# A value projection between a tile's scores and their product, and a modulation step at the end of tile 0, in the mLSTM and retention heads

## The reference, cut to what matters

```python
qk = jnp.einsum('nbhtd,nbhsd->nbhts', qc, kc)                  # scores of a block
s = qk_c * jnp.exp(d_c - m_t[..., None])                       # mLSTM: scores times decay
num = einsum(s, v_c) + w_inter * einsum(q_c, C)                # product with the values, plus the carried state
C = dec * C + einsum(kw, v_c)                                  # the state takes in keys times values
o_intra = einsum(einsum(q, k) * dec_intra, v)                  # retention: the same with constant decays
mod = cs @ w_ada[l] + b_ada[l]                                 # modulation, one vector per layer and condition
```

## Time and profile before

| | |
|---|---|
| Time, median of 3 executions | 1649.74 us (1644.46 to 1652.1) |
| Profiled execution, its own time | 1651.91 us |
| Its span, first to last instruction | 1650.1 us |
| PE busy | 1537.0 us, 93% |
| DVE busy | 961.3 us, 58% |
| ACT busy | 627.9 us, 38% |
| Mean granted PE clock | 0.967 |

### The profile page before, as it was taken

How to read it: one execution, slowest core, us unless ns; L and a number is a source line. 1 busy time by engine, 2 the same in 40 slices (tenths; PEclk the granted TensorE clock), 3 DMA queues, 4 the chain that set the end, 5 groups by cost and what they waited for, 6 DMA issues and landing times. The chain is left out here.

```text
span 1650.1 us, 30954 instructions
## 1 busy us (share of the span) xinstructions
PE 1537.0 (93%) x11168; PEld 1433.2 (87%) x11168; DVE 961.3 (58%) x2118; ACT 627.9 (38%) x1491; POOL 181.0 (11%) x384
## 2 busy tenths in 40 slices
PE   6999999998999999899799999899999999977898
PEld 2689898987999999799698889889999999966898
DVE  2565555554766656643565555576677677663622
ACT  2522222222232222332554434254555555543521
POOL 1000000000000000000100010022223122312000
PEclk8999999999999999999899899999999999988999
DMA  9434333432551433133342213221111211020223
GB/s 326 116 100 104 95 104 94 109 88 48 126 153 46 140 95 109 48 99 92 118 81 73 67 43 80 73 65 47 50 48 43 70 43 54 5 72 2 89 87 115
DMA packets 195257, 140.89 MB, mean 85 GB/s; under 512 B 18332, under 2 KB 178584, under 8 KB 194916
## 3 DMA queue, kind: packets, MB, share of 16 engines
q1 hardware_dynamic: 177772, 130.16, 28.2%
q10 hardware_dynamic: 17400, 9.60, 2.0%
HBM read 128.58 MB, written 11.15 MB: 85 GB/s over the span
## 5 line engine op out<-in xcount | busy, mean ns | idle before, releaser
L180 PE MATMUL bank<-hT,w_high 128*128 128x288 f32 x1152 | 364.4, 316 | 6.7 <-ACT gla_ls_x L1195 2.4
L181 PE MATMUL bank<-hT,w_low 128*128 128x288 f32 x1152 | 345.6, 300 | 0.0
L182 PE MATMUL bank<-hT,w_high 128*128 128x288 f32 x1152 | 345.2, 300 | 0.0
L180 PEld LDWEIGHTS bank<-hT,w_high 128*128 128x128 f32 x1152 | 223.3, 194 | 9.0 <-ACT gla_ls_x L1195 2.6
L181 PEld LDWEIGHTS bank<-hT,w_low 128*128 128x128 f32 x1152 | 223.2, 194 | 0.0
L182 PEld LDWEIGHTS bank<-hT,w_high 128*128 128x128 f32 x1152 | 222.5, 193 | 0.0
L180 PE MATMUL bank<-output_w_split,gT_high 128*128 128x256 f32 x512 | 143.4, 280 | 0.0
L182 PE MATMUL bank<-output_w_split,gT_high 128*128 128x256 f32 x512 | 143.2, 280 | 0.0
L181 PE MATMUL bank<-output_w_split,gT_low 128*128 128x256 f32 x512 | 142.5, 278 | 0.0
L181 PEld LDWEIGHTS bank<-output_w_split,gT_low 128*128 128x128 f32 x512 | 96.8, 189 | 0.0
L180 PEld LDWEIGHTS bank<-output_w_split,gT_high 128*128 128x128 f32 x512 | 96.1, 188 | 0.1
(11 more groups left out here) (487 smaller groups left out, 3597.4 us busy)
## 6 DMA issues: line engine op xcount, KB each, us to landing
x<-in_w_in_even SPq DMA_DIRECT2D x72, 512.0 KB, 5.0
x<-in_w_in_odd SPq DMA_DIRECT2D x56, 512.0 KB, 4.1
x<-in_w_ada SPq DMA_DIRECT2D x32, 256.0 KB, 4.5
front_w_ada<-in_w_ada SPq DMA_DIRECT2D x6, 1024.0 KB, 14.8
output_w_raw<-in_w_out_even SPq DMA_DIRECT2D x12, 512.0 KB, 3.4
output_w_raw<-in_w_out_odd SPq DMA_DIRECT2D x12, 512.0 KB, 3.6
gdn_E<-G_rows SPq DMA_DIRECT2D x8, 576.0 KB, 5.0
gT<-in_w_ada SPq DMA_DIRECT2D x16, 256.0 KB, 4.0
```

The lines of the kernel that those rows point to most:

```text
L180: pe.matmul(out, w[0], x[1], start=first, stop=False)
L181: pe.matmul(out, w[1], x[0], start=False, stop=False)
L182: return pe.matmul(out, w[0], x[0], start=False, stop=last)
```

## The change

There are two edits. On PE, in tile 0 of an mLSTM head the value projection moves behind the scores and transposes, and in the first of these heads behind `pe_columns` as well. In a retention head the value projection of tile 0 stays, and that of tile 1 moves up from the beginning of tile 1 to the place behind the scores of tile 0; kind C is as before. On DVE, in a retention head the later step at the end of tile 3 is now at the end of tile 0. Steps are counted as they are issued, so step 4 is now the one at the end of tile 0, and steps 5, 6 and 7 take the places of 4, 5 and 6.

```diff
                         if t == 0:
                             project_gates(t)
                             pe.wait_ge(*v_low.done(h, NC - 1))
-                            project_v(t)
+                            if kind != "A":
+                                project_v(t)
                             if kind == "A" and previous is None:
                                 chain.pe_columns(pe)
                             pe.wait_ge(*(qk_copied.done(h, NP - 1) if kind == "A" else qk_ready.done(h, 0)))
-                        else:
+                        elif t > 1 or kind != "B":
                             project_v(t)
                         pe.wait_ge(*kw_ready.before(h, t))
...
                         last.then_inc(scores_psum.sem, 1)
+                        if t == 0 and kind != "C":
+                            project_v(1 if kind == "B" else 0)
                         if t:
                             project_gates(t)
...
-                        if kind == "B" and t == PT - 1:
+                        if kind == "B" and t == 0:
                             later_step(h)
```

## The result

The changed kernel took 1639.65 us (median of 8 executions, 1636.72 to 1641.2) against 1647.62 for the kernel before (8 executions, 1644.46 to 1652.1). The medians differ by 8.0 us. The ratio of the two kernels, which is not taken from these two medians, is 0.9946, with a 95% interval of 0.9936 to 0.9956: 8.9 us faster (7.2 to 10.5). Timed again in another job (the experiment before the last) it was 0.9934, 0.9920 to 0.9947: 10.9 us (8.7 to 13.2), with medians 12.2 apart. The forecast was 1638.7 and a gain of 11.0. The profiled execution took 1638.62, with a span of 1636.8 us.

What follows compares the result with a forecast made beforehand. PE, busy 93% of the span, was taken as the bound, so only its stalls and slow clock counted. Terms 3.3 + 4.4 + 0.4 + 2.9 = 11.0 us, off the median 1649.74, gave 1638.7, range 1635 to 1645.

Steps and rivals of the forecast that it cites:

- Retention, tile 0: Product of tile 0, four heads: tile 1's value matmuls fill PE's wait for the scores; 3.3 us gained.
- The new wait for ACT's copy: Retention tile 0: the moved projection overwrites bank 3 and waits for ACT's copy of the values; costs 0.08 per head.
- Retention, tile 1: Moved step on DVE ahead of tile 1's scores costs nothing, with 0.7 us of cover before the product.
- A flush behind the step: DVE after the moved step: by the skill page about 0.95 us more, overrunning cover by 0.25 a head; gain 10, not 11.
- The loads: Weight blocks of steps 4 to 7, needed about one tile earlier, still land in time; nothing is late.
- The rival of a late block: Retention: step 4's block has not landed when DVE needs it; 5 us late would give 1656; chance 0.03.
- Retention, tile 4: Product of the sample tile, four heads: its wait for v_sample goes once the step is moved; 4.4 us gained.
- mLSTM, heads 2 to 4: Product in tile 0: the wait for scores becomes one for ACT's value copy; 0.13 a head, 0.4 us gained.
- PE's reaction to ACT: PE's delay after the end of ACT's copy, taken as 0.09 us in sizing the waits on copied values.
- mLSTM, first head, directly: Product's wait stays at nearly 2 us because the load of negM bounds the chain; only 0.2 us gained.
- mLSTM, first head, the clock: A dense value block ahead of the wait keeps PE's higher clock level behind it; 2.7 us gained.
- the forecast's first rival: First mLSTM head: the clock still falls because the wait keeps its length; gain 8.3, 1641.4 us; chance 0.26.

Runs made afterwards that it cites:

- e2: Kernel before with only the retention value projection of tile 1 moved ahead of tile 0's product, later step left at tile 3: 1645.42 us, ratio 0.9970.
- e5: Changed kernel with two later steps at the end of tile 0 of a retention head and none in tile 1: 1642.38 us, ratio 0.9958 to the kernel before.
- e3: Kernel before with only the retention later step moved from the end of tile 3 to the end of tile 0, PE order unaltered: 1644.19 us, ratio 0.9967.
- e9: Changed kernel, unaltered, timed again beside the kernel before on the same chip: 1638.53 us against 1650.69, ratio 0.9934.
- e8: Kernel before, unaltered, profiled once more: 1645.48 us in its one execution.
- e1: Kernel before with only the mLSTM edit, tile 0's value projection behind the scores in all mLSTM heads: 1647.35 us, ratio 0.9986.
- e4: Kernel before with the new PE order in the first mLSTM head only: 1647.99 us, ratio 0.9992.
- e6: Changed kernel with mLSTM tile 0 also in retention order and ACT copying tile 0's values before the decays: 1633.93 us, ratio 0.9904 to the kernel before.

## Why the prediction was right, point by point

- **Retention, tile 0 (forecast 3.3).** Right. In the first head, from the scores of tile 0 to the product of tile 1 it was 10.00 before and is 442.01 - 432.79 = 9.22: 0.78, forecast 0.77. The other heads had idles of up to 0.7 before, and e2 shows 0.9 a head, 3.6 in all (0.1 of it was not in the forecast: in the first head the value block of tile 2 takes 443.45 to 446.26, 2.81, instead of 2.91, and why is open). The new wait for ACT's copy is there: the first value matmul starts 0.64 behind the start of the scores, against 0.59 without a wait.
- **Retention, tile 1 (nothing).** Right. The scores of tile 1 are done at 441.04, PE sees it by 441.24, and the product stands at 442.01: 0.77 of cover by the rows, 0.82 by e5, forecast 0.7.
- **A flush behind the step.** The successor of the moved step starts after 1.32 us of its 1.41, and after both pairs in e5 at 2.65 of 2.73. By the Trainium skill, VectorE: DVE Perf Modes, section "The DRAIN you can't avoid", a flush of about an operation's duration less 266 ns would have stood there. The trace after doesn't agree with the forecast's estimate from it, for at 0.95 more the product would have waited, and it did not. The same section adds that a next operation that is not held starts earlier, which the estimate left out; so this pair need not contradict it.
- **The loads (nothing).** Right. DVE went from `g` straight to the step, 0.41 apart, with no wait for a block. The rival of a late block is out.
- **Retention, tile 4 (4.4).** Right: 1.94 became 0.86, and e3 shows 1.2 a head, 4.8 in all. The three retention terms together were 7.7; the start of the heads moved from 402.06 to 399.07 and their last transposes from 685.79 to 674.58, so they gave 8.2. Most of the 0.5 more is the 0.1 a head named under tile 0.
- **mLSTM, heads 2 to 4 (0.4).** The mechanism was right, the size half of it. The wait moved to `mlstm_v` with an idle of 0.56. From the first gate matmul to the product the third head took 9.79 before and 9.72 after, the fourth 9.80 and 9.73: 0.07 a head, 0.2 in all. The step that was mis-sized is PE's reaction to ACT, taken as 0.09 from the first head. In the third head (ACT, then PE):

```profile
265.47 0.38 ACT L1247 ACTIVATE mlstm_v<-bank 128x256 f32<-128x256 f32 x1 [2.89 <-PE bank L182]
266.00 0.67 PE L173 MATMUL bank<-mlstm_v,mlstm_scores 128*128 128x257 f32 x2 [0.56 <-ACT mlstm_v L1247]
```

  PE's last value matmul began at 265.16, so a next one could have begun at 265.28; the copy started 0.19 later, where the forecast had 0.20, and took its 0.38. PE then began 0.15 after its end instead of 0.09, and that is the missing 0.06.
- **mLSTM, first head, directly (0.2).** 12.80 from the gates to the product became 12.69: 0.1, and 12.55 in e9, 0.3. The load bounded it, as forecast.
- **mLSTM, first head, the clock (2.7).** Right for the profile that the forecast read: 6.90 became 4.20. It was the least certain term, and it is shown by comparison: all four profiles in which the small transposes and scores stand right ahead of the wait (before, e2, e3, e8) have a fall to the 1.2 GHz level there, after an idle of 2.06. None of the five with the 24 value matmuls between them and a wait of 1.79 to 2.00 has one (after, e1, e4, e5, e9). That the gap alone lowers the clock, the forecast's first rival, does not fit: the gap stayed and the clock did not fall. That the wait is also 0.06 us shorter in e4 was not taken apart from the order.
- **The sum.** By the traces the change gave 2.8 in the first head, 8.2 in retention and 0.2 in mLSTM heads 2 to 4, so 11.2 against the forecast's 11.0; retention gave more than forecast and the other terms less. The timed gains, 8.9 and 10.9, are about 1 us less on average; 11.0 lies outside the interval of the first (7.2 to 10.5) and inside that of the second. One part is seen: in e8 the clock of the kernel before falls for a shorter time, and there is 1.0 us less to win. The two profiled spans differ by 13.3, but 2.1 of this lie behind the retention heads (957.0 and 954.9), where nothing was changed.
- **The time itself.** That 1639.65 came so near to 1638.7 is in part luck. The forecast started from a median of three executions, 1649.74; over eight it is 1647.62, 2.1 lower. By medians the gain was 8.0, 3.0 less than forecast, and the two differences nearly cancel.

## What to carry to other kernels

When PE waits for a short piece of another engine's work, put a block between its inputs and its use that is independent of both, and then check the tile that comes next: in retention the later product had 0.8 us of room, in kind C it had none and the wait only changed its name. A late load that can't be hurried was better covered by the next tile's work (e6, 1.9 us more in the first head, with ACT's copy moved ahead as well) than by the same tile's (0.1). Where several small gains are added up, take the length of a repeated stage as the ruler, since a median carries the scatter of stages that were not touched.

## What the hardware showed that was not expected

- The same wait of 2.06 us, with the same instructions ahead of it, came with a lower clock that began in the wait in three profiles (at about 100.4 in the first, by the 0.72 of the earlier trace rows) and lasted 6.8 us, and that began 1.3 us behind its end in e8 and lasted 3.4 us. What decides that stays open.
- In the second mLSTM head PE waits for ACT, which waits for a weight block from memory, and the length of that wait changes from one execution to the next, whatever the kernel. ACT's row in e3 and in the changed kernel:

```profile
165.61 1.06 ACT L973 ACTIVATE mlstm_w_v_high<-x 128x1024 fp32r<-128x1024 f32 x1 [5.21 <-DMA x<-in_w_in_even]
```

```profile
162.81 1.06 ACT L973 ACTIVATE mlstm_w_v_high<-x 128x1024 fp32r<-128x1024 f32 x1 [3.79 <-DMA x<-in_w_in_even]
```

  The row behind it on PE waited 1.65 us in the one and 0.23 in the other: the 1.42 by which the block came later. That is more than the direct gain in the four mLSTM heads, and enough to hide a part kernel's gain in e4. Why the block is late in some executions was not tried.
